# Differential attention on Trainium2: wide projection pairs, a tail interleaved with the last heads, and VectorE's order at three places

## What is computed

```
proj = h @ w_in                                  # 1024 -> 3072: queries, keys, values
q, k = rms_norm of each 64-wide group, times a gain
p1, p2 = softmax(q1 @ k1.T + bias), softmax(q2 @ k2.T + bias)      # 8 heads, two maps each
out = (p1 - lam * p2) @ v                        # 8 heads of 128 columns
out = rms_norm(out, subln_g) * (1 - lam_init);  x = x + out @ w_out
```

## Time and profile before

| | |
|---|---|
| median of 3 runs | 1393.77 us (1389.6 to 1393.89) |
| the profiled execution | 1387.45 us, its span 1385.6 us |
| mean granted clock of TensorE | 0.994 of full speed |
| stretch of diff's projections | 704 to 767 us of the span |
| stretch of diff's heads and tail | 767 to 830 us |
| ffn3's two context steps | about 926 to 953 us |
| border from ffn1 to ffn2 | about 504 to 530 us |

### The profile page before, as it was taken

The page is one execution under the profiler, slowest core; times in us unless marked ns, Lnnn a source line. Parts: engine busy times, 40 slices in busy tenths (PEclk is TensorE's granted clock), DMA queues, the critical chain, the costliest instruction groups (busy, mean ns, idle before and its releaser), DMA issues.

```text
span 1385.6 us, 19422 instructions
## 1 busy us (share of the span) xinstructions
PE 1359.6 (98%) x7989; PEld 1185.8 (86%) x7989; DVE 971.3 (70%) x1134; ACT 725.3 (52%) x978; POOL 116.5 (8%) x173
## 2 busy tenths in 40 slices
PE   8999999999999999999999999999999999999998
PEld 7888889878888889888899878888888868888887
DVE  6788876966687777777776857566576775765564
ACT  6444457445544445444465755544455455644443
POOL 2100000200000000000023012000014002100000
PEclk9999999999999999999999999999999999999999
DMA  9877545424877647887555326554543212365551
GB/s 293 295 246 254 202 141 184 145 91 148 307 245 244 227 166 252 272 276 256 193 180 183 125 92 230 189 201 159 196 124 126 57 33 92 120 214 185 199 193 61
DMA packets 171959, 256.16 MB, mean 185 GB/s; under 512 B 4884, under 2 KB 145471, under 8 KB 168671
## 3 DMA queue, kind: packets, MB, share of 16 engines
q1 hardware_dynamic: 169534, 248.63, 53.2%
q0 software_dynamic: 2176, 6.24, 1.8%
q10 hardware_dynamic: 160, 0.05, 0.0%
HBM read 253.59 MB, written 1.32 MB: 184 GB/s over the span
## 4 chain that ended last, share of the span: by engine, by line
PE 58%; DVE 3%; ACT 2%; issue 1%; POOL 0%; DVEq 0%; POOLq 0%; ACTq 0%
PE acc L224 15%; PE banks L615 15%; PE banks L625 8%; PE banks L186 3%; PE banks L187 3%; PE banks L188 3%; PE banks L575 2%; PE banks L605 1%; DVE w_lo L177 1%; PE banks L2474 1%; ACT w_hi L171 1%; PE acc L2393 1%; PE banks L2418 1%; DVE arena L313 1%; PE banks L2542 0%
## 5 line engine op out<-in xcount | busy, mean ns | idle before, releaser
L177 DVE TENSOR_TENSOR w_lo<-w_raw,w_hi 128x2048 fp32r<-128x2048 f32 x212 | 486.9, 2298 | 130.3 <-ACT w_hi L171 129.5
L171 ACT ACTIVATE w_hi<-w_raw 128x2048 fp32r<-128x2048 f32 x212 | 404.8, 1909 | 52.2 <-PE acc L224 17.2
L615 PE MATMUL banks<-h_both,w_hi 128*128 128x512 f32 x1520 | 371.2, 391 | 1.3 <-issue 1.3
L615 PEld LDWEIGHTS banks<-h_both,w_hi 128*128 128x128 f32 x1520 | 278.7, 188 | 55.5 <-issue 3.0
L625 PEld LDWEIGHTS banks<-h_both,w_lo 128*128 128x128 f32 x1520 | 194.9, 191 | 7.4
L625 PE MATMUL banks<-h_both,w_lo 128*128 128x256 f32 x1520 | 197.2, 283 | 0.0
L224 PE MATMUL acc<-w_lo,act_hi 128*128 128x512 f32 x400 | 155.9, 390 | 0.0
L224 PE MATMUL acc<-w_hi,act_hi 128*128 128x512 f32 x400 | 155.8, 390 | 0.0
L224 PE MATMUL acc<-w_hi,act_lo 128*128 128x512 f32 x400 | 155.8, 390 | 0.0
L471 ACT ACTIVATE silu_gate<-banks 128x512 f32<-128x512 f32 x55 | 32.9, 598 | 150.9 <-PE banks L615 133.8
L485 ACT ACTIVATE act_hi<-act 128x512 fp32r<-128x512 f32 x50 | 31.5, 630 | 138.7 <-PE acc L224 138.7
(11 more groups left out here) (350 smaller groups left out, 1956.4 us busy)
## 6 DMA issues: line engine op xcount, KB each, us to landing
w_raw<-in_ffn_w_gu SPq DMA_DIRECT2D x88, 1024.0 KB, 5.2
w_raw<-in_ffn_w_down SPq DMA_DIRECT2D x44, 1024.0 KB, 4.8
arena<-in_w_ada SPq DMA_DIRECT2D x24, 1024.0 KB, 5.3
w_raw<-in_w_ffn_in SPq DMA_DIRECT2D x22, 1024.0 KB, 5.1
w_raw<-in_gla_w_in SPq DMA_DIRECT2D x12, 1024.0 KB, 5.2
w_raw<-in_diff_w_in SPq DMA_DIRECT2D x12, 1024.0 KB, 5.1
w_raw<-in_w_ffn_out SPq DMA_DIRECT2D x11, 1024.0 KB, 4.8
w_raw<-in_w_in SPq DMA_DIRECT2D x9, 1024.0 KB, 5.2
```

The source lines that it names most:

```text
L171: eng.activation(w_hi[:, slot, :], w_raw[:, slot, :], ACT.Copy).then_inc(sem("unit_hi"), 1)
L177: eng.tensor_tensor(w_lo[:, slot, :], w_raw[:, slot, :], w_hi[:, slot, :].bitcast(F32), ALU.subtract).then_inc(sem("unit_split"), 1)
L615: return pe.matmul(outs[ct], hi[:, k, ct * P:(ct + 1) * P], h_both[:, k, :, t], start=k == 0, stop=k == KT - 1)
```

## The change

Projection: units 0 to 9 become five pairs of 512 columns. Each of a pair's two units now holds half the depth (4 of 8 steps) of both former units' columns. A pair is four half-depths of 12 products of 512 columns: first half of the depth for tile 0 and tile 1, then the second half for both; a tile has a bank of its own. Copies out of the banks, squares, sums and scales go by tile of a pair. On DVE the first tile's sum is followed at once by its scale, with no split between. The four transposed copies of a pair (two units) come together: queries after the next pair, keys inside the next pair before its last half-depth.

Tail: `out_turned(0)` moves into head 6, `out_turned(1)` and the first tile of unit 12 into head 7 ahead of that head's product with the values; ACT's and DVE's lists follow; `keep_warm` goes.

DVE's order: at the two ada borders the pick comes after the first two residual additions and the columns after the last `norm_low`; in ffn3 the four modulations come before the split of the step's third unit, the low parts stay after it.

`gla_tile_done` is renamed `tile_done` and shared. Core of the diff:

```diff
@@ -525,6 +525,9 @@
...
         eng.tensor_tensor(lo, act_tiles, hi.bitcast(F32), ALU.subtract).then_inc(sem("act_lo_ready"), 1)
+        if next_stage(name) == "mix" and i in (5, 6):
+            eng.wait_ge(sem("ada_columns"), 14)
+            ctx_full_vector(eng, i - 5)
         if i < NI - 1:
...
@@ -541,8 +544,7 @@
...
-                eng.wait_ge(sem("ada_columns"), 12)
-                ctx_half_vector(eng, i - 5)
+                ctx_low_vector(eng, i - 5)
...
-    for j in range(N_DIFF_IN):
+    for p in range(DIFF_PAIRS):
+        for deep in range(2):
+            load_unit(sp, u + 2 * p + deep, w[:, 4 * deep:4 * deep + 4, p * 2 * UC:(p + 1) * 2 * UC])
+    for j in range(2 * DIFF_PAIRS, N_DIFF_IN):
         load_unit(sp, u + j, w[:, :, j * UC:(j + 1) * UC])
...
+    def pair_tile(p, t):
+        if t:
+            eng.wait_ge(sem("unit_used"), u + 2 * p + 2)
+        else:
+            eng.wait_ge(sem("tile_done"), 4 + p + 1)
+        n = 2 * p + t
+        eng.activation(diff_wide[:, p, t, :], diff_bank(p, t), ACT.Copy).then_inc(sem("diff_copied"), 1)
+        if p < 4:
+            eng.wait_ge(sem("diff_copied"), n + 1)
+            if n >= 2:
+                eng.wait_ge(sem("diff_sums"), n - 1)
+            eng.activation(diff_sq[:, t, :], diff_wide[:, p, t, :], ACT.Square).then_inc(sem("diff_squared"), 1)
+    def queries(n):
+        eng.wait_ge(sem("diff_transposed"), n + 1)
...
+        eng.activation(diff_q[:, 2 * n:2 * n + 2, :].rearrange("p h t -> p (h t)"), acc_bank[n], ACT.Copy,
+                       scale=diff_qg[:, :]).then_inc(sem("diff_q_ready"), 1)
...
-    for j in range(10):
-        unit(j)
...
+    split_hi(eng, u + 3)
+    for p in range(DIFF_PAIRS):
+        pair_tile(p, 0)
+        pair_tile(p, 1)
+        split_hi(eng, u + 2 * p + 4)
+        if 1 <= p < 3:
+            queries(2 * p - 2)
+            queries(2 * p - 1)
+        if p < DIFF_PAIRS - 1:
+            split_hi(eng, u + 2 * p + 5)
...
@@ -1258,22 +1291,28 @@
...
         eng.activation(diff_pt[:, h % 2, :], bank[h % 2][:, :], ACT.Copy).then_inc(sem("diff_pt_ready"), 1)
+        if h == 6:
+            high(0)
         if h >= 2:
             squares(h - 2)
         if h == 5:
             unit(11)
+    high(1)
     squares(DH - 2)
-    high = lambda *pairs: mixer_split_scalar(eng, name, lambda b: diff_og[:, :], pairs)
-    high(0, 1)
+    split_hi(eng, u + N_DIFF_IN + 2)
     squares(DH - 1)
-    split_hi(eng, u + N_DIFF_IN + 2)
+    high(2)
     split_hi(eng, u + N_DIFF_IN + 3)
-    high(2, 3)
+    high(3)
     border_scalar(eng, name)
...
+    def group_sums(n):
+        eng.wait_ge(sem("diff_squared"), n + 1)
+        eng.tensor_reduce(ssq[:, n * per_unit:(n + 1) * per_unit],
+                          diff_sq[:, n % 2, :].rearrange("p (g d) -> p g d", d=DDH), AX.X, ALU.add)\
             .then_inc(sem("diff_sums"), 1)
...
+    def group_scale(n):
+        eng.wait_ge(sem("diff_rstd"), n + 1)
+        g = diff_wide[:, n // 2, n % 2, :].rearrange("p (g d) -> p g d", d=DDH)
+        r = rstd[:, n * per_unit:(n + 1) * per_unit]
+        eng.tensor_tensor(g, g, r.unsqueeze(2).broadcast_to([P, per_unit, DDH]), ALU.mult)\
             .then_inc(sem("diff_scaled"), 1)
...
+    split_lo(eng, u + 3)
+    for p in range(4):
+        group_sums(2 * p)
...
+        group_scale(2 * p)
+        if p == 3:
+            keys(0)
+            keys(1)
+        group_sums(2 * p + 1)
+        split_lo(eng, u + 2 * p + 4)
+        group_scale(2 * p + 1)
+        split_lo(eng, u + 2 * p + 5)
     keys(2)
...
     for h in range(DH):
         if h + 1 < DH:
             logits(h + 1)
         combine(h)
+        if h == DH - 1:
+            split_at(0)
         if h >= 1:
             output(h - 1)
...
+    split_at(1)
+    normed(2)
     output(DH - 1)
...
-    split_at(0)
-    normed(2)
-    split_at(1)
+    split_lo(eng, u + N_DIFF_IN + 2)
     normed(3)
-    split_lo(eng, u + N_DIFF_IN + 2)
+    split_at(2)
     split_lo(eng, u + N_DIFF_IN + 3)
-    split_at(2)
     split_at(3)
     border_vector(eng, name, 1.0)
...
+    def wide_product(p, kk, t, h, low):
+        w = (w_lo if low else w_hi)[:, (u + 2 * p + kk // 4) % RING, :].rearrange("p (k c) -> p k c", k=4)
+        last = kk == KT - 1 and (low if (p, t) == (0, 0) else h is h_lo)
+        return pe.matmul(diff_bank(p, t), h[:, kk, S + t * P:S + (t + 1) * P], w[:, kk % 4, :],
+                         start=kk == 0 and h is h_hi and not low, stop=last)
+    def half_depth(p, deep, t, arriving=False):
+        pe.wait_ge(sem("unit_split"), u + 2 * p + deep + 1)
+        for kk in range(4 * deep, 4 * deep + 4):
+            if arriving and kk % 2 == 0:
+                pe.wait_ge(sem("h_ready"), h0 + t * KT + kk + 2)
+            wide_product(p, kk, t, h_hi, False)
+            wide_product(p, kk, t, h_hi, True)
+            last = wide_product(p, kk, t, h_lo, False)
+        return last
+    def first_pair():
+        half_depth(0, 0, 0, True)
...
+            if kk % 2 == 0:
+                pe.wait_ge(sem("h_ready"), h0 + kk + 2)
+            if kk == 6:
+                norm_turn(pe, name, 1)
             for h in (h_hi, h_lo):
...
+                wide_product(0, kk, 0, h, False)
         pe.wait_ge(sem("unit_split"), u + 2)
...
+        for kk in range(4, KT):
+            last = wide_product(0, kk, 0, h_hi, True)
+        last.then_inc(sem("tile_done"), 1)
+        half_depth(0, 0, 1, True).then_inc(sem("unit_used"), 1)
+        half_depth(0, 1, 1, True).then_inc(sem("unit_used"), 1)
+    def wide_pair(p):
+        if p >= 2:
+            pe.wait_ge(sem("diff_copied"), 2 * p - 2)
+        half_depth(p, 0, 0)
+        half_depth(p, 0, 1).then_inc(sem("unit_used"), 1)
+        half_depth(p, 1, 0).then_inc(sem("tile_done"), 1)
+        if p >= 3:
+            turned(2 * p - 2)
+            turned(2 * p - 1)
+        half_depth(p, 1, 1).then_inc(sem("unit_used"), 1)
+        if p < 3:
+            turned(2 * p - 2)
+            turned(2 * p - 1)
...
             last_unit_part(h)
+        elif h == 6:
+            out_turned(0)
+        else:
+            out_turned(1)
+            project_rows(0, 0)
         pe.wait_ge(sem("diff_pt_ready"), h + 1)
+        if h == 0:
+            pe.wait_ge(sem("diff_copied"), 2 * DIFF_PAIRS + 1)
         if h == 6:
...
     ada_taken(pe, name)
...
-    for j in range(2, 10):
-        unit(j)
-        turned(j - 2)
+    first_pair()
+    for p in range(1, DIFF_PAIRS):
+        wide_pair(p)
     scores(0)
...
-    for h in range(DH):
-        head(h)
     def out_turned(b):
         pe.wait_ge(sem("diff_normed"), b + 1)
-        pe.wait_ge(sem("diff_o_copied"), DH - 1 + b // 2)
+        if b == 0:
+            pe.wait_ge(sem("diff_copied"), N_DIFF_IN)
+        elif b < 3:
+            pe.wait_ge(sem("diff_pt_ready"), 6 + b)
+        else:
+            pe.wait_ge(sem("diff_o_copied"), DH)
...
-    def project(n):
+    def project_rows(n, t):
+        if n == 0 and t == 0:
+            pe.wait_ge(sem("diff_maxed"), 4 * DH)
         ready(n)
-        add_rows(pe, u + N_DIFF_IN + n, tiles(n), n == 0)
-    out_turned(0)
-    out_turned(1)
-    keep_warm(pe, 12, 3)
-    project(0)
+        pe.wait_ge(sem("unit_split"), u + N_DIFF_IN + n + 1)
+        for half in range(2):
+            mm = row_quarter(pe, u + N_DIFF_IN + n, tiles(n), t, half, n == 0, False)
+        if t == TT - 1:
+            mm.then_inc(sem("unit_used"), 1)
+    for h in range(DH):
+        head(h)
+    project_rows(0, 1)
     out_turned(2)
-    project(1)
+    project_rows(1, 0)
+    project_rows(1, 1)
     out_turned(3)
     last_rows(pe, name, lambda n: tiles(2 + n), lambda n: ready(2 + n))
...
-    ada_pick_vector(eng, block)
+    eng.wait_ge(sem("ada_columns"), 1 if block == 1 else 10)
...
+def ctx_full_vector(eng, half):
+    mod = ada_col[:, 1]
     for k in range(4 * half, 4 * half + 4):
         if k % 2 == 0:
             eng.wait_ge(sem("ctx_transposed"), k // 2 + 1)
         eng.tensor_scalar(h_full[:, k, :], ctx_place(k), mod[:, 0, k:k + 1], mod[:, 1, k:k + 1], ALU.mult,
                           ALU.add).then_inc(sem("h_full_ready"), 1)
-        if k % 4 >= 2:
-            low(k - 2)
-    low(4 * half + 2)
-    low(4 * half + 3)
+def ctx_low_vector(eng, half):
+    h0 = h_ready_before("mix")
+    for k in range(4 * half, 4 * half + 4):
+        eng.wait_ge(sem("h_hi_ready"), h0 + k + 1)
+        eng.tensor_tensor(h_lo[:, k, 0:S], h_full[:, k, :], h_hi[:, k, 0:S].bitcast(F32), ALU.subtract)\
+            .then_inc(sem("h_ready"), 1)
...
@@ -2813,11 +2921,11 @@
...
-    if ada_block_before(following) in (1, 2):
-        ada_columns_vector(eng, ada_block_before(following))
     split_lo(eng, base[following])
     residual(eng, name, 0, 0, scale)
     residual(eng, name, 0, 1, scale)
+    if ada_block_before(following) in (1, 2):
+        ada_pick_vector(eng, ada_block_before(following))
     norm_scale(eng, following, 0)
     residual(eng, name, 1, 0, scale)
```

(38 more changed lines are left out.)

86 lines of the change are left out of this document (28 added, 58 removed).

## The result

The changed kernel took 1376.63 us in the median of four runs (1376.22 to 1376.97), beside 1393.83 for the kernel before on the same chip: a ratio of 0.9878, 95% interval 0.9865 to 0.9892. That is 17.2 us less, where 8.3 were forecast, and 2.9 us under the low end of the range. Its profiled execution took 1376.54 us for a span of 1374.7, at its median; the one of before took 1387.45, 6.4 us under its median. So the profiles differ by 10.9 us only, and nearly all of the other 6.3 lies between executions of the kernel before itself.

The account below looks back on a forecast made before the run. TensorE, busy 98% of the span, was taken as the bound. Pairs 2.5, tail 3.7, border 0.8 and context steps 1.3 sum to 8.3 us, taking the median from 1393.77 to 1385.5; range 1379.5 to 1390.

Parts of the forecast that it names:

- Tail: Tail of diff, heads 6 and 7: filling two waits and dropping the warm-up saves 3.7 us, bounds 2 to 4.2.
- Pairs: Diff's projections: five pairs with 512-column products save 2.5 us, bounds 0 to 3.
- rivals A: Diff's projection pairs: VectorE, not TensorE, sets the pace, so the pairs save nothing; 5.8 us saved, 1388.0; chance 0.12.
- D: Diff's projections: both waits of a pair uncovered make VectorE the bottleneck, 13 us over four pairs; slower, 1398.5; chance 0.03.
- the sign named for them: Diff's projections: waits of the turned copies on VectorE's scale would show the forecast wrong; no size given.
- Border: Border from ffn1 to ffn2: starting the split 1.1 us earlier closes TensorE's wait; 0.8 us saved, bounds 0.3 to 1.0.
- Context steps: ffn3's two context steps: modulations moved into VectorE's idle time remove TensorE's waits; 1.3 us saved, bounds 1.0 to 1.5.
- The sum of 8.3: Whole kernel: savings of 2.5, 3.7, 0.8 and 1.3 us add to 8.3, bounds 3.3 to 9.7.
- rival C: Tail of diff: head 7's half unit and unit 14 wait for inputs; 6.4 us saved or less, 1387.4 to 1389; chance 0.10.
- Rival B: Tail of diff: the clock falls because the warm-up is gone; 6.6 us saved, 1387.2; chance 0.10.
- The range: Whole kernel: savings of 4 to 10 give 1384 to 1390; a median 4.2 us lower extends it to 1379.5 to 1390.

Follow-up runs that it names:

- the kernel that suffered most: The changed kernel with the tail of before: median 1387.34 us; with the gate's blocks also set between the mix stage's narrow products, 1379.56 us.

## Why the prediction was right and wrong

**The parts were right.** Tail: 3.7 forecast, 4.0 measured; the wait before head 6's product fell from 1.21 to 0.77, head 7's was filled, the warm-up went, and the low part came 0.28 us ahead of TensorE where 0.3 were worked out. Pairs: 2.5 forecast, 2.6 measured; the rate was 227 ns rather than 232, but the wait on unit 1's low part (0.29) and one on the keys (0.32, forecast as within 0.5 of ready) took that back. The 2.5 thus came out partly by errors that cancel. VectorE kept pace: rivals A and D did not come, though the sign named for them, the turned copies waiting on VectorE's scale, showed once, for these 0.32 us. Border: 0.8 forecast, 0.94 measured. Context steps: 1.3 forecast, 1.84 measured, over the bound of 1.5, because the listed idle was taken for the whole hole. The sum of 8.3 was 9.4, inside its bounds of 3.3 to 9.7. Nor did rival C: units 12 and 14 found their low parts made. Rival B, the clock in the tail, did not come: 1.00 from 763 to 822 us after. Windows of the kernel after, for the earlier trace rows:

```profile
703.00:763.50 60.50, 59.76 (x282) 48.85 (x280) 43.19 (x58) 35.28 (x47) 26.24 (x24) 1.00 0.57 188
763.50:822.50 59.00, 56.39 (x375) 48.23 (x375) 45.54 (x137) 44.05 (x128) 7.31 (x11) 1.00 0.33 112
```

**The step that failed** is the last of the sum: "Median: 1393.77 - 8.3 = 1385.5", with the sentence ahead of it, "I work out a difference on the profile and take it from the median". It took the 6.3 us between the profiled execution and the median for something that the changed kernel would carry too. They are 20.48 us at 1.2 GHz in the mix stage in place of one stretch of 3.41, which by their clock and time 50 of 119 runs of the kernel before have and none of ten of the changed kernel. The profile shown held four short stretches and the earlier trace rows gave one of them a price of 1.7 us, but the clock was only asked about where the change edits. The range had the same fault: it let the median fall by the 4.2 us that the lowest of the three runs shown lay lower, not by the 6.3 of the profiled execution, though that is a run of the same kernel. From that execution the measured sum gives 1387.45 - 9.4 = 1378.0; the 1.5 us left over, put down to the fall at 1150 us, make it 1376.5.

So of the 17.2 us first measured, 9.4 are the work of the change, 1.5 a short fall fewer in the profile, and 6.3 the long fall. The size of the last is in part chance: three of the first four runs of before were long, where 50 of 119 are. Over all runs the medians are 1387.64 and 1376.70, 10.9 us apart. How much of the last two a later edit gives back depends on where it moves the mix stage: 0.46 us of added work brought some of it.

## What to carry to other kernels

Before a difference is subtracted from a median, ask why the profiled execution and the median differ: list the granted clock of every run, and see whether the times lie in groups. An edit that moves a later stage can win or lose more through the clock there than through its own work, so compare landmarks ahead of the first such fall, and judge parts by traces and not by medians. Where stretches of narrow products stand alone, set full products between them; it costs about half a microsecond here and takes 7.8 off the median of the kernel that suffered most, and it gains nothing in the changed kernel where it stands (1376.89 beside 1376.74).

## What was not expected of the hardware

The clock fell to 1.2 GHz while TensorE was busy 10.00 of 10 us, after 3.3 us mostly of products of 40 and 64 rows, and stayed there for 20.48 us; three profiles show it, each from the same place of the program. The same program did this in some executions and not in others. Adding 0.93 us of work to the kernel before lowered its median by 3.2 us.
